# Four groups of tiles moved to other distances, modulo 512 bytes, from the TensorE weights in SBUF

## What is computed

```python
def swiglu_ffn(h, w_up, w_down):
    a, b = jnp.split(h @ w_up, 2, axis=-1)
    return (jax.nn.silu(a) * b) @ w_down

for l in range(DEPTH):                      # first_block
    x = x + 0.5 * swiglu_ffn(rmsnorm(x, ffn1_norm[l]), ffn1_w_up[l], ffn1_w_down[l])
    x = x + mixer(rmsnorm(x, mix_norm[l]), ...)
    x = x + 0.5 * swiglu_ffn(rmsnorm(x, ffn2_norm[l]), ffn2_w_up[l], ffn2_w_down[l])
    x = rmsnorm(x, final_norm[l])
...
for l in range(DEPTH):                      # second_block
    ...
    x = x + mix @ w_o[l]
    h = rmsnorm_2(x, norm2[l])
    up = dwconv_centred(h @ w_up[l], conv_w[l], conv_b[l])
    gate, val = up[..., :D_FF_2], up[..., D_FF_2:]
    x = x + (jax.nn.silu(gate) * val) @ w_down[l]
```

## The kernel before

| group | tiles in it that TensorE reads in `mm3` | distance |
|---|---|---|
| after the weights | `x`, `h_hi`, `h_lo`, `sq` | 192 |
| at_a | `s_*`, `f_*`; also `qk`, `xsq`, `psq` | 192 |
| at_v | `hid_*`; also `v`, `silu_t`, `prod_t`, `up_t` | 192 |
| at_u | `n_*`, `yt_*`, `g_*`; also `upad` | 192 |
| behind upad | none; `cv`, `gate`, `bv`, `spread` | 128 |
| at_t | `last_*`, `end_*`; also `z`, `zt`, `p_sb`, `pt_sb` | 192 |

## Time and profile before

### The profile page before, as it was taken

How to read it: one execution, slowest core, us unless ns; L and a number is a source line. 1 busy time by engine, 2 the same in 40 slices (tenths; PEclk the granted TensorE clock), 3 DMA queues, 4 the chain that set the end, 5 groups by cost and what they waited for, 6 DMA issues and landing times.

```text
span 1957.0 us, 38879 instructions
## 1 busy us (share of the span) xinstructions
PE 1910.4 (98%) x15828; PEld 1841.5 (94%) x15828; DVE 1471.9 (75%) x2159; ACT 1104.8 (56%) x1414; POOL 41.9 (2%) x52
## 2 busy tenths in 40 slices
PE   7999999999999999999999999999999999999998
PEld 7999898799999999998988999999889999889998
DVE  6555799987765585558999877555888777878777
ACT  5444666576644464446666765444665655656554
POOL 0000011000000000000110000000000000000000
PEclk9999999999999999999999999999999999999999
DMA  6556599634555545555996446555335554435554
GB/s 251 202 178 224 190 290 272 185 99 148 208 201 185 192 172 196 183 214 183 292 279 173 107 141 217 202 184 184 130 109 196 208 193 156 141 119 192 193 193 153
DMA packets 62731, 368.57 MB, mean 188 GB/s; under 512 B 8096, under 2 KB 8352, under 8 KB 25888
## 3 DMA queue, kind: packets, MB, share of 16 engines
q1 hardware_dynamic: 54704, 339.37, 49.7%
q0 software_dynamic: 6912, 25.17, 7.2%
q10 hardware_dynamic: 1008, 2.51, 0.3%
HBM read 359.68 MB, written 1.05 MB: 184 GB/s over the span
## 4 chain that ended last, share of the span: by engine, by line
PE 74%; DVE 17%; ACT 4%; DMA 3%; issue 2%; SPq 0%; DVEq 0%; ACTq 0%
PE bank L447 23%; PE bank L448 23%; PE bank L449 22%; DVE lo L1651 5%; DVE cv L1899 4%; ACT hi L1070 1%; DVE zt L1862 1%; DMA zt<-zt 1%; DMA lo<-in_w 1%; PE bank L626 1%; PE bank L653 1%; ACT n_hi L1132 1%; PE bank L639 1%; PE bank L611 1%; DVE qk L1864 0%
## 5 line engine op out<-in xcount | busy, mean ns | idle before, releaser
L1651 DVE TENSOR_TENSOR lo<-raw,hi 128x2048 fp32r<-128x2048 f32 (+1 forms) x336 | 663.5, 1976 | 200.8 <-ACT hi L1070 200.1
L1070 ACT ACTIVATE hi<-raw 128x2048 fp32r<-128x2048 f32 (+1 forms) x336 | 598.7, 1784 | 108.8 <-PE bank L449 98.0
L447 PE MATMUL bank<-n_hi,hi 128*128 128x256 f32 x2256 | 637.9, 283 | 20.8 <-DVE lo L1926 11.5
L448 PE MATMUL bank<-n_lo,hi 128*128 128x256 f32 x2256 | 631.4, 280 | 0.0
L449 PE MATMUL bank<-n_hi,lo 128*128 128x256 f32 x2256 | 631.3, 280 | 0.0
L447 PEld LDWEIGHTS bank<-n_hi,hi 128*128 128x128 f32 x2256 | 430.8, 191 | 26.7 <-DVE lo L1926 11.5
L448 PEld LDWEIGHTS bank<-n_lo,hi 128*128 128x128 f32 x2256 | 424.9, 188 | 1.3 <-issue 1.0
L449 PEld LDWEIGHTS bank<-n_hi,lo 128*128 128x128 f32 x2256 | 425.1, 188 | 0.0
L447 PE MATMUL bank<-h_hi,hi 128*128 128x256 f32 x1152 | 330.8, 287 | 7.0 <-DVE h_lo L1655 3.9
L449 PE MATMUL bank<-h_hi,lo 128*128 128x256 f32 x1152 | 321.5, 279 | 0.0
L448 PE MATMUL bank<-h_lo,hi 128*128 128x256 f32 x1152 | 321.5, 279 | 0.0
(11 more groups left out here) (263 smaller groups left out, 2317.8 us busy)
## 6 DMA issues: line engine op xcount, KB each, us to landing
raw<-in_w SPq DMA_DIRECT2D x286, 1024.0 KB, 4.9
raw<-in_w SPq DMA_DIRECT2D x53, 512.0 KB, 4.0
lo<-in_w POOLq DMA_DIRECT2D x48, 512.0 KB, 9.1
zt<-zt SPq DMA_DIRECT2D x96, 64.0 KB, 6.9
bv<-in_bv SPq DMA_DIRECT2D x2, 768.0 KB, 6.1
spread<-in_spread SPq DMA_DIRECT2D x2, 768.0 KB, 7.9
x<-in_x ACTq DMA_DIRECT2D x4, 256.0 KB, 10.2
out_x<-sq SPq DMA_DIRECT2D x1, 1024.0 KB, 3.9
```

Source lines behind the costliest of these rows:

```text
L447: mm(out, w_hi, a_hi, start=start, stop=False, skip_group_check=True)
L448: mm(out, w_hi, a_lo, start=False, stop=False, skip_group_check=True)
L1070: fn(hi[:, s, 0:w], raw[:, s, 0:w], ACT.Copy).then_inc(sem["hi"], 1)
L1651: v.tensor_tensor(lo[:, s, 0:w], raw[:, s, 0:w], hi[:, s, 0:w].bitcast(F32), ALU.subtract)\
```

## The change

Three paddings are put into the layout and one is taken out. The tiles of at_a move up by 256 bytes, those of at_v by 640, those of at_u and the ones behind `upad` by 1088, those of at_t by 1024. No instruction is added, removed or moved on any engine; only addresses in SBUF differ. 1024 bytes more of each partition are used.

```diff
+    state["at"] += 256
     at_a = state["at"]
     qk = sb("qk", [P, 24, S], F32)
     s_hi = sb("s_hi", [P, KT, S], F32R, at_a)
     s_lo = sb("s_lo", [P, KT, S], F32R, at_a + KT * S * 4)
+    state["at"] += 384
     at_v = state["at"]
     v_sb = sb("v", [P, 2, GROUPS * 512], F32)
     hid_hi = sb("hid_hi", [P, 2, S], F32R, at_v)
...
     psq = sb("psq", [P, KT, S], F32, at_a)
+    state["at"] += 448
     at_u = state["at"]
     upad = sb("upad", [P, KT, UPW], F32)
     n_hi = sb("n_hi", [P, KT, S], F32R, at_u)
...
-    state["at"] += 64
     at_t = state["at"]
     z = sb("z", [P, 2, S], F32)
```

## The result

The changed kernel took 1987.59 us (median of four executions, 1986.04 to 1990.78) against 1951.82 us for the kernel before (four, 1948.0 to 1954.49): ratio 1.0167, 95% interval 1.0135 to 1.02. Compared again later, six executions against eleven of before in between, it was 1985.85 against 1961.86 us, ratio 1.0124 (1.0097 to 1.0152). The changed kernel repeats within 7 us, the kernel before spreads over more than 20 us (1947.35 to 1971.21 beside these experiments); why is part of what follows. One execution of the kernel before, slow at 8221.03 us, is left out of every comparison. Forecast were 1924.4 us, and a range of 1914 to 1966.

The account below looks back on a forecast made before the run. In the FFN loops TensorE bounds: matmul count times distance between starts. First block's FFNs going to 113 ns, -27.4 us, plus projections lost, +2.6, gave -24.8: 1949.2 - 24.8 = 1924.4 us, range 1914 to 1966.

Parts of the forecast that it names:

- Step 1: Work of the other engines, such as VectorE's conv multiply-adds at 477 ns: the moved addresses cost nothing there.
- Step 2: Matmuls at stake: 6768 on n_*, 2784 on hid_*, 384 on s_*; four of six FFNs run at 118 ns.
- step 3: Price of a changed pace: 7.1 us per FFN; first block's four FFNs 27.4 us, second block's two 12.5, projections 2.6.
- Step 4: Pace at the new distances: first block's FFNs go to 113 ns, second block's keep theirs; bounds -34 to +15 us.
- A third pace: n_* and hid_* matmuls at 122 ns, another 4.5 ns slower: +58 us in all, up to 2007 us; chance 8%.
- The one on the other side: Slower: second block's loops lose 113 ns as n_* and hid_* distances differ; +15 us, 1964; chance 20%.
- the addresses don't matter: Rule from the Trainium skill on TensorE's reads and weight loads, set against the forecast: time stays at 1949 us.
- The projections: Matmuls on s_* and yt_* (384 + 192), now at 113.4 ns, counted as losing 4.5 ns each: +2.6 us.

Follow-up runs that it names:

- The version that beats both: Kernel before, with the first half of each FFN's first down chunk (24 matmuls) reading hid_* values from their own tile at distance 256; 1939.34 us, ratio 0.9886.

## Why the prediction was wrong, step by step

**The bound was right.** TensorE without a wait in the loops, the two paces of 113.3 and 117.8 ns, and that a pace is taken on at an interruption and then held: all of it was seen again. The runs add that a change of distance sets it too, without an interruption, and the versions with eight added matmuls and with the tile of its own use that.

**Step 1 was right.** The conv multiply-adds took 479 ns against 477 before, 1 us in all, and VectorE's busy time rose by 1.2 us.

**Step 2 and the price of step 3 were right.** One loop is worth 7 us. The version that beats both has all six at 113 ns and is 1961.86 - 1939.34 = 22.5 us below the kernel before, three loops' worth; the profiled execution of before had four at 118 ns, and the others don't all have four.

**Step 4 failed: which pace the new distances give.** It said that "a distance doesn't set a new pace but decides into which of two the stream falls", took 113 ns for the first block's FFNs, and let the second block's keep theirs. The runs show that a distance does set the paces: two at 192 and 448, one at the others (at 64 nearly always), 117.9 ns at 320 and 120.0 ns at 256, so that all six loops went to a mean of 119.3 ns. I had one near row, the turned matmuls at 320, saw 118 and 113 ns there, and carried it over to 320 and from there to 256 and 448, for which there was no row, as the text itself said. `hid_*` at 320 never took 113 ns in the three traces that have it there. Whether the turned roles are another case isn't shown: `n_*` at 64, the same place modulo 256, did take 113 ns, but seldom. Nine steps can show that a pace occurs, not that a loop will run at it.

The premise beside it was misread as well. "The restart that always led to 118 ns", behind the sum of squares, was seen in the fourth FFN and taken for all four. In the first FFN of the same trace that restart, at 23.3 us, led to 113 ns, which was held until an interruption between a down chunk and the next up chunk:

```profile
24.24 0.28 PE L447 MATMUL bank<-n_hi,hi 128*128 128x256 f32 x1
...
25.37 0.28 PE L448 MATMUL bank<-n_lo,hi 128*128 128x256 f32 x1
...
38.48 0.28 PE L449 MATMUL bank<-hid_hi,lo 128*128 128x256 f32 x1
38.76 0.36 PE L447 MATMUL bank<-n_hi,hi 128*128 128x256 f32 x1
...
39.08 0.28 PE L449 MATMUL bank<-n_hi,lo 128*128 128x256 f32 x1
...
40.25 0.28 PE L447 MATMUL bank<-n_hi,hi 128*128 128x256 f32 x1
```

Ten steps take 1.13 us in front and 1.17 us behind. So no one restart set the pace of the four FFNs, and "I expect them to go together" stood on a single one; they did go together, because distance 256 leaves no choice.

**The reason for choosing 113 ns was none.** "They can only stay or gain" supposed that 118 ns was the upper end. A third pace stood among the bounds, but at 122 ns and with 8%, because no row showed it. With 120.0 for `n_*` and 117.9 for `hid_*` the sum of step 3 would have been +31 us in place of -24.8, and near the measured +24 to +36. The unknown had bounds of -34 and +58 us; the range should have taken in the second one with more than it did, since nothing in the trace excluded it.

**The rivals.** The one on the other side had the sign, but another mechanism (a pace lost at each change between unequal tiles), and the run with `hid_*` alone at 320 shows that it isn't so: `n_*` kept 113 ns through two loops beside `hid_*` at 320. That the addresses don't matter, which the prediction took from the Trainium skill, fails too. The same instruction stream at the same granted clock takes 120.0 ns per matmul with both tiles at 256, and 113.3 or 117.8 ns with both at 192. The Trainium skill, "TensorE: Matmul & The Clock Gate", section "Step-by-step: what each phase is for", says that loading the next weights doesn't take read bandwidth from the running matmul; for these fp32r matmuls of 256 columns, with a new weight tile each, the measurement speaks against it, since moving the weights `lo` alone changed the pace from 120.0 to 117.8 ns. That it is read bandwidth that is lost stays an inference; no row shows the reads.

**The projections.** Counted as lost with 2.6 us; `s_*` at 448 lost nothing, `yt_*` at 256 lost 1.2 us.

## What to carry to other kernels

Where TensorE streams matmuls with a new weight load for each, compare the distance between starts across stretches of the same shape before anything else: a difference at the same granted clock was here a matter of where the tiles stand and of what the stream did before, and no engine's wait shows it. For an address never tried, the trace of before gives no price: measure a map first, one group of tiles at each distance in one run. And where one kernel's times spread wider than another's, look for a pace or an order that is left to chance; fixing it (here 24 matmuls in each FFN read from another place) gave 1.1%, more than any of the layouts tried, of which the best gave 0.2%.

## What was not expected of the hardware

- A 256-column fp32r matmul with its weight load takes 113.3, 117.8, 118.6 or 120.0 ns by the distance between the moving tile and the weight tile modulo 256 bytes: 120.0 at 0, 117.8 (seldom 113.3) at 64, 118.6 at 128, 113.3 or 117.8 at 192.
- At 192 the stream holds either of two paces for hundreds of matmuls. Coming from whole chunks at distance 256 it took 113 ns at every change of tile; 24 matmuls at 256 turned 118 into 113 ns in six FFNs of six, eight added ones in the three of six that came at 118.
- Moving `lo` alone by 64 bytes took the same moving tiles from 120.0 to 117.8 ns; moving everything by 64 bytes, and `n_*` by 256 more, did nothing.
- The order is that of 256 columns: with 512 columns, the chunk moving against `n_*`, distance 256 has the lower mean step, 227 ns against 229 to 230.
